# Eleven places where TensorE multiplies the identity once to three more times

## The reference

```python
def second_block(x, c, ada_w, ada_b, w_in, ...):
    cond = jax.nn.silu(c)
    for layer in range(DEPTH_2):
        mod = (jnp.dot(cond, ada_w[layer]) + ada_b[layer])[:, None, :]
        sh1, sc1, g1, sh2, sc2, g2 = jnp.split(mod, 6, axis=-1)
        u = x * (1.0 + sc1) + sh1
        mix = _mixer(u, w_in[layer], conv_w[layer], gk_w2[layer], gk_b[layer],
                     gla_norm_w[layer], w_out[layer])
        x = _layernorm(DEEPNORM_ALPHA * x + (1.0 + g1) * mix, ln1_g[layer], ln1_b[layer])
        u = x * (1.0 + sc2) + sh2
        j = layer // 2
        if layer % 2 == 0:
            ff = _dense_swiglu(u, ffn_w_gate[j], ffn_w_up[j], ffn_w_down[j])
        else:
            ff = _moe_swiglu(u, router_w[j], moe_w_gate[j], moe_w_up[j], moe_w_down[j])
        x = _layernorm(DEEPNORM_ALPHA * x + (1.0 + g2) * ff, ln2_g[layer], ln2_b[layer])
    return x
```

```python
    gk = jax.nn.log_sigmoid((jnp.einsum("bsr,rk->bsk", g_low, gk_w2) + gk_b).astype(jnp.float32))
    gk = jnp.maximum(gk / GATE_NORMALIZER, GATE_LOG_MIN)
    ...
    b = jnp.cumsum(gk.astype(jnp.float32).reshape(shp_k), axis=2)
```

## Time and profile before

| what | value |
|---|---|
| three timed runs | 2050.76, 2058.37, 2059.92 us |
| median | 2058.37 us |
| time of the profiled execution | 2051.38 us |
| its span, first to last instruction | 2049.6 us |
| TensorE busy | 1951.5 us (95%) |
| VectorE busy | 649.2 us (32%) |
| ScalarE busy | 170.3 us (8%) |
| TensorE's mean granted clock | 0.986 |
| memory traffic | 656 MB, mean 320 GB/s |

### The profile page before, as it was taken

One profiled execution on the slowest core, in us unless ns is written; L12 is line 12 of the kernel. 1 busy time (PEld: TensorE's weight loads), 2 busy tenths in 40 slices (PEclk: granted clock), 3 DMA queues, 4 the chain that ended last, 5 costly groups with the idle time before them and its releaser, 6 DMA issues.

```text
span 2049.6 us, 68398 instructions
## 1 busy us (share of the span) xinstructions
PE 1951.5 (95%) x31337; PEld 1567.6 (76%) x31337; DVE 649.2 (32%) x1411; ACT 170.3 (8%) x369; POOL 17.3 (1%) x66
## 2 busy tenths in 40 slices
PE   6999999999999989999999999998999999999996
PEld 4787468777777857648776577588999989989895
DVE  5586333222222232164332523530011110111104
ACT  2002010000000002000000110010000000000000
POOL 1000000000000000000000000000000000000000
PEclk9999999999999999999999999999999999999998
DMA  9998559999999995327766733279999999999992
GB/s 350 314 389 330 214 215 397 420 422 423 421 421 425 420 398 213 142 77 276 261 213 233 267 109 123 103 289 392 411 389 413 405 406 415 403 413 406 405 364 114
DMA packets 179139, 656.00 MB, mean 320 GB/s; under 512 B 16212, under 2 KB 20724, under 8 KB 170868
## 3 DMA queue, kind: packets, MB, share of 16 engines
q1 hardware_dynamic: 170528, 647.41, 80.5%
q0 software_dynamic: 1456, 5.24, 0.7%
q10 hardware_dynamic: 7076, 2.20, 0.5%
HBM read 653.76 MB, written 1.05 MB: 319 GB/s over the span
## 4 chain that ended last, share of the span: by engine, by line
PE 90%; DVE 5%; DMA 3%; issue 2%; SPq 0%; DVEq 0%; ACT 0%
PE ps L1844 88%; DMA ring<-in_moe_w_gate_dram 2%; PE ps L1852 1%; DMA ring<-in_w_ada_dram 1%; DVE stat L1103 0%; DVE arena L1508 0%; DVE arena L1303 0%; DVE hT L991 0%; DVE x L1212 0%; DVE tok L978 0%; DVE tok L1211 0%; DVE newton L971 0%; DVE hT L1086 0%; DVE x L1097 0%; DVE arena L1177 0%
## 5 line engine op out<-in xcount | busy, mean ns | idle before, releaser
L1844 PE MATMUL ps<-arena,ring 128*64 128x80 f32 (+2 forms) x25216 | 877.5, 230 | 23.2 <-issue 18.1
L1844 PEld LDWEIGHTS ps<-arena,ring 128*64 128x64 f32 (+1 forms) x25216 | 859.8, 138 | 50.3 <-issue 40.4
L1844 PE MATMUL ps<-hT,ring 128*128 128x256 f32 (+1 forms) x1680 | 359.4, 385 | 4.2 <-DVE stat L995 2.2
L1844 PEld LDWEIGHTS ps<-hT,ring 128*128 128x128 f32 (+1 forms) x1680 | 308.2, 189 | 51.0 <-issue 2.5
L1844 PE MATMUL ps<-ring,arena 128*64 128x512 f32 (+1 forms) x880 | 273.8, 595 | 1.5 <-DVE stat L1774 1.1
L1844 PE MATMUL ps<-arena 128*128 128x128 f32 (+6 forms) x1576 | 209.1, 307 | 14.0 <-DVE arena L1711 5.6
L1844 PEld LDWEIGHTS ps<-ring,arena 128*64 128x64 f32 (+1 forms) x880 | 104.5, 159 | 150.8 <-issue 147.2
L1844 PEld LDWEIGHTS ps<-arena 128*128 128x128 f32 (+4 forms) x1576 | 138.3, 166 | 67.6 <-issue 31.1
L1469 DVE MEMSET ps<- 128x480 f32 x68 | 28.9, 425 | 278.5 <-ACT arena L742 273.6
L1844 PE MATMUL ps<-ring,hT 128*128 128x512 f32 (+2 forms) x256 | 87.6, 500 | 0.0
L1844 PEld LDWEIGHTS ps<-ring,hT 128*128 128x128 f32 x256 | 46.1, 190 | 38.1 <-issue 36.2
(11 more groups left out here) (325 smaller groups left out, 797.9 us busy)
## 6 DMA issues: line engine op xcount, KB each, us to landing
ring<-in_moe_w_gate_dram SPq DMA_DIRECT2D x128, 704.0 KB, 8.0
ring<-in_moe_w_up_dram SPq DMA_DIRECT2D x128, 704.0 KB, 9.2
ring<-in_moe_w_down_dram SPq DMA_DIRECT2D x176, 512.0 KB, 10.5
ring<-in_w_gate_dram SPq DMA_DIRECT2D x32, 2048.0 KB, 14.8
ring<-in_w_up_dram SPq DMA_DIRECT2D x32, 2048.0 KB, 14.1
ring<-in_w_down_dram SPq DMA_DIRECT2D x32, 2048.0 KB, 12.3
ring<-in_w_in_dram SPq DMA_DIRECT2D x19, 2048.0 KB, 13.9
ring<-in_w_ada_dram SPq DMA_DIRECT2D x12, 2048.0 KB, 15.7
```

The costliest lines, as they stand in the source:

```text
L1844: ins = pe.matmul(*args, **kw)
```

## The change

`keep_busy` is called in eight more executed places, and its count is raised from 3 to 5 in three more. Nothing is removed and no other instruction is moved.

- after `token_transposes` of the first sub-layer, ahead of `hT_ready(1)`: 2
- ahead of the second `token_transposes` (it waits for `tokens_normed`): 3; after it, ahead of `hT_ready(2)`: 1
- inside `tile_transposes`, three calls: 5 in place of 3
- ahead of `hT_ready(5)`, the start of layer 1: 1; ahead of `hT_ready(4)` and `hT_ready(6)`: 1 each
- in both mixers, ahead of the wait for `gk_ready`: 3 each

```diff
@@ -2040,6 +2040,7 @@
             pe.wait_ge(consts_ready, 1)
             pe.wait_ge(H["tokens_normed"], 1)
             token_transposes(tok)
+            keep_busy(2)
             hT_ready(1)
@@ -2166,8 +2167,10 @@
             ada_product(1, 8)
             ada_turn(1, 7, bank, 4).then_inc(v_full, 1)
+            keep_busy(3)
             pe.wait_ge(H["tokens_normed"], 2)
             token_transposes(tok)
+            keep_busy(1)
             hT_ready(2)
             pe.wait_ge(got_router, 80)
@@ -2496,7 +2499,7 @@
-            FILL = (3, 3)
+            FILL = (5, 5)
@@ -2534,6 +2537,8 @@
                     last.then_inc(v_full, 1)
+                if layer:
+                    keep_busy(1)
                 hT_ready(3 + 2 * layer)
```

## The result

The change makes the kernel slower. Thirteen runs of it have a median of 2076.58 us (2060.67 to 2099.80), thirteen of the kernel before 2056.34 us (2050.76 to 2064.65). The medians stand 20.2 us apart. The prediction was 2051.5 us in a range of 2043.5 to 2061.0: a small gain where there is a loss.

What follows compares the result with a forecast made beforehand. The prediction took the kernel as bound by TensorE's list with short waits. 9.25 us from the clock less 5.4 at the gates gave 3.85 us less, from the 2055.1 us mean 2051.3, taken as 2051.5 us; range 2043.5 to 2061.0.

Steps and rivals of the forecast that it cites:

- What bounds the kernel: Whole kernel: a TensorE list with short waits, TensorE busy 1951.5 of 2049.6 us; time changed between waits moves everything behind.
- The slower one: Rival at the two `gk_ready` waits: filling paid, clock falls as before; 5.4 us more, 2060.5 us; chance 0.10.
- The cost of a filling: Identity products on TensorE at full clock: 0.94 us for one, 1.84 for two, 2.74 for three.
- Nine places without a cost: Nine of the eleven filled places have a wait longer than the filling, so the cost there is nothing.
- The gates, 5.4 us,: Decay gates of both mixers, ahead of `gk_ready`: no wait there, so three products each cost 2 x 2.7 = 5.4 us.
- What the clock gives back: Stretches at 0.50 behind filled waits return to full clock, saving 9.25 us; bounds 0 to 12.6.
- the five stretches: Slow-clock stretches at 45.3, 253.5, 926.0, 1175.1 and 1325.3 us: savings of 1.65, 1.55, 2.83, 1.67 and 1.55 us.
- The terms of the tile transposes, 6.05 us: Stretches at 926.0, 1175.1 and 1325.3 us behind the tile transposes: savings of 2.83, 1.67 and 1.55 us.
- as they are: Slow stretches at 1236.6 and 2014.8 us follow waits the change doesn't fill; no saving or cost was counted.
- The sum up to the second experts: Net of the clock's 9.25 us saving and the gates' 5.4 us cost: 3.85 us less.
- The rule on transposes: Skill's rule that full clock doesn't engage for transposes; by it stretches at 253.5 and 1325.3 us would stay slow.
- The rival built on the rule of the Trainium skill: Transposes don't hold the clock at 253.5 and 1325.3 us: 3.1 us stays lost, net 0.75 less, 2054.4 us; chance 0.15.

Runs made afterwards that it cites:

- 21 dead products alone: Kernel before plus 21 identity products in the never-taken dense branch of the first experts, nothing more executed: median 2086.41 us, against 2057.96 for the kernel before.
- the loop put back: Changed kernel plus 43 identity products in the never-taken branch, 64 with its own 21: median 2056.08 us, ratio to before 0.9981.
- 0, 10, 32 and 53 dead products: Kernel before with that many identity products in the never-taken branch; medians with 10, 32 and 53: 2058.82, 2054.96 and 2060.19 us.
- the fastest kernel: Changed kernel without the gates' fillings, two products ahead of each `gla_in` wait, 45 products in the never-taken branch: median 2042.60 us, ratio 0.9928.

## Why the prediction was wrong

- **What bounds the kernel.** The step that failed is the first: "time saved or added on TensorE between two waits should move everything behind it". It reckons with what is executed alone. Added code also moves code, and here it moved a loop of 6.3 blocks to a place where it is fetched again: about 12 us an episode and 20 us in the median. The same place costs 28 us in the median with nothing executed (21 dead products alone: 2086.41 us against 2057.96). The place of the code was a term that the sum put at nothing, without a reason. None of my rivals had it. The slower one had 5.4 us of another mechanism. A sign of it stood in the page of before: "issue" at 2% of the chain. Most of TensorE's part of it, 19.7 us, lies in the second experts, at the jumps and in the loop's first turns.
- **The cost of a filling** was right: 2.74 to 2.84 us for three and 4.46 for five.
- **Nine places without a cost** was right: in each the wait that is left is 0.2 to 1.4 us, and from the work ahead of each wait to the work behind it no more than 0.1 us was added.
- **The gates, 5.4 us,** was right in kind: 2 x 2.58 = 5.2 us in the trace, 4.5 us alone (1.0 to 8.0).
- **What the clock gives back.** Four of the five stretches vanished in after; the fifth, of 10.1 us, shrank to one that begins behind the router, at the 16 transposes of `find_slots` (3.63 us). The products that I had counted are at the lengths that I had taken. The terms of the tile transposes, 6.05 us, measured 6.4 (3.9 to 9.1). That the stretches behind the 2.78 us waits would stay "as they are" was a mis-sized term: before's trace has such a stretch behind one of the two waits, after's behind both, and the one at 1235.5 us is 9.8 us long.
- **The sum up to the second experts.** Predicted 3.85 us less, measured 1.9 us more in the profiled executions. The difference is 5.7 us. What I left alone cost 7.2 us more than in before: 3.1 us behind the wait at 834.58 us (the state products and features), 3.0 behind the one at 1235.51 us, where 4.99 us stand against 3.19 and 30.27 against 29.06, and 1.1 behind the first experts. About 1.5 us came back where the filled places gave more than my terms. With the loop put back the change measures 0.9981, and that this is my 3.85 us is in part luck: the interval reaches from 0.2 to 7.6 us, and in the two profiled executions the same sum missed by 5.7.
- **The rule on transposes.** In after the stretch 253.5 to 260.2 us, with transposes, one filling and a router, is at 1.00, where it was at 0.50:

```profile
253.50:260.20 6.70, 5.67 (x85) 4.70 (x86) 3.30 (x18) 3.91 (x7) 2.94 (x3) 1.00 1.01 405
```

Three products ahead of the transposes and one behind them were enough, and the router of layer 1 ran at full clock too (2.04 us). The rival built on the rule of the Trainium skill ("TensorE: Matmul & The Clock Gate", Part 4: PE-mode transpose) did not come about in this trace; whether transposes alone would do is not shown.

## What to carry to other kernels

Before adding instructions to a program with a long loop, look at the instruction queue and at idle time put down to "issue" at the loop's jump: if the count of instruction transfers rises with an edit, the loop has moved to a bad place, and dead code in a branch that is never taken can put it back and shows whether that is the cause. Take several runs of it, since at a bad place one execution can still be fast (2050.22 us). Fill waits only where the trace has a wait: the same idea cost 4.5 us (1.0 to 8.0) at the gates, and at the next wait of the same mixer it saved 6.1 us in the traces of two executions, 4.3 us in the medians. And compare an edit with a control that has the same code size, or the placement's 20 to 28 us hide a term of 4.

## What the runs showed of the hardware

TensorE's code comes in transfers of 16 KB (61 transfers, 1.00 MB). A loop of about 6.3 such blocks ran without fetches after its first turns at 0, 10, 32 and 53 dead products, and was fetched again in two or three turns at 16, 21 and 85 and in six at 27, at 9 transfers and about 10 to 12 us an episode: 5.0 to 8.3 us at the jump, shorter stands behind, and (read in after) TensorE at 1.2 GHz behind the long one. It fits a store that holds seven blocks of the loop but not eight; that is an inference from the band, not measured by itself. The same binary ranges over 50 us from run to run at a bad place (2050.22 to 2102.53) and over 13 us at a good one (2045.94 to 2058.81).

The spread of the kernel before, whose cause the prediction left open, goes with the clock. Of 23 runs the fastest (2048.39 us) has a mean granted clock of 0.987 and the slowest (2064.66 us) one of 0.980. As an estimate, 0.007 less on the mean is 1.4% of the time at 0.50, 29 us, in which half the work is lost: 14 us, of the 16 between the two. In the fastest kernel, where the two waits for `gla_in` are filled as well, the spread is 3.2 us.
